# Two of the five wide combine passes of the sample stage on GpSimd instead of VectorE

## The reference

```python
def combine_patterns(outs, lses):
    w = jax.nn.softmax(jnp.stack(lses, axis=0), axis=0)
    return jnp.sum(w[..., None] * jnp.stack(outs, axis=0), axis=0)
```

## Time and profile before

| | |
|---|---|
| Runs | median 3155.96 us of 3 (3154.74 to 3160.87) |
| Profiled execution, its own time | 3153.91 us |
| Its span in the trace | 3152.2 us |
| Busy: PE, DVE, ACT, POOL | 91%, 39%, 28%, 6% of the span |

### The profile page before, as it was taken

One profiled execution on the slowest core, in us unless ns is written; L12 is line 12 of the kernel. 1 busy time (PEld: TensorE's weight loads), 2 busy tenths in 40 slices (PEclk: granted clock), 3 DMA queues, 4 the chain that ended last, 5 costly groups with the idle time before them and its releaser, 6 DMA issues. The chain is left out here.

```text
span 3152.2 us, 49398 instructions
## 1 busy us (share of the span) xinstructions
PE 2876.6 (91%) x17770; PEld 1632.3 (52%) x17770; DVE 1235.5 (39%) x2977; ACT 887.1 (28%) x2188; POOL 192.6 (6%) x476
## 2 busy tenths in 40 slices
PE   7998887673989898996997999999999999999998
PEld 6655665452657474765443444444444444444444
DVE  6326555564646465564443222222112221122134
ACT  6116666222434343443222110111001210011111
POOL 2000000100112020211110000000000000000000
PEclk9999889886989898997998999999999999999999
DMA  5121222752010201102322102111231112311035
GB/s 179 75 93 39 81 61 58 225 172 65 15 49 8 56 16 42 34 10 78 138 93 80 40 20 110 41 40 40 88 131 41 40 40 93 127 41 40 33 126 177
DMA packets 177965, 231.40 MB, mean 73 GB/s; under 512 B 12561, under 2 KB 141924, under 8 KB 177148
## 3 DMA queue, kind: packets, MB, share of 16 engines
q1 hardware_dynamic: 173142, 216.53, 21.4%
q0 software_dynamic: 4656, 12.65, 1.3%
HBM read 160.08 MB, written 69.07 MB: 73 GB/s over the span
## 5 line engine op out<-in xcount | busy, mean ns | idle before, releaser
L2312 DVE TENSOR_TENSOR f_hidden<-f_silu,f_ps_up 128x512 f32<-128x512 f32 (+1 forms) x110 | 65.2, 593 | 627.5 <-ACT f_silu L2253 627.5
L113 PE MATMUL f_ps_gate<-act_hi,f_w_hi 128*128 128x512 bf16 (+1 forms) x880 | 285.5, 343 | 11.1 <-DVE f_w_lo L2299 9.5
L113 PE MATMUL f_ps_y<-f_down_hi,f_h_hi 128*128 128x512 bf16 (+1 forms) x748 | 284.3, 380 | 8.5 <-issue 6.4
L114 PE MATMUL f_ps_gate<-act_lo,f_w_hi 128*128 128x512 bf16 (+1 forms) x880 | 285.4, 343 | 0.0
L115 PE MATMUL f_ps_gate<-act_hi,f_w_lo 128*128 128x512 bf16 (+1 forms) x880 | 285.2, 343 | 0.0
L114 PE MATMUL f_ps_up<-act_lo,f_w_hi 128*128 128x512 bf16 (+1 forms) x880 | 284.6, 342 | 0.0
L115 PE MATMUL f_ps_up<-act_hi,f_w_lo 128*128 128x512 bf16 (+1 forms) x880 | 284.6, 342 | 0.0
L113 PE MATMUL f_ps_up<-act_hi,f_w_hi 128*128 128x512 bf16 (+1 forms) x880 | 284.6, 342 | 0.0
L114 PE MATMUL f_ps_y<-f_down_lo,f_h_hi 128*128 128x512 bf16 (+1 forms) x748 | 284.3, 380 | 0.0
L115 PE MATMUL f_ps_y<-f_down_hi,f_h_lo 128*128 128x512 bf16 (+1 forms) x748 | 284.1, 380 | 0.0
L2253 ACT ACTIVATE f_silu<-f_ps_gate 128x512 f32<-128x512 f32 (+1 forms) x110 | 57.1, 519 | 656.6 <-PE f_ps_up L115 656.6
(11 more groups left out here) (360 smaller groups left out, 5483.0 us busy)
## 6 DMA issues: line engine op xcount, KB each, us to landing
y_part_rows<-f_total SPq DMA_DIRECT2D x48, 512.0 KB, 2.6
f_total<-y_part_rows SPq DMA_DIRECT2D x48, 512.0 KB, 3.5
f_raw_gate<-in_w_gate SPq DMA_DIRECT2D x22, 512.0 KB, 4.5
f_raw_up<-in_w_up SPq DMA_DIRECT2D x22, 512.0 KB, 5.9
f_raw_down<-in_w_down SPq DMA_DIRECT2D x22, 512.0 KB, 3.6
m_w_raw<-in_w_in SPq DMA_DIRECT2D x20, 512.0 KB, 5.1
s_comb<-pattern_rows SPq DMA_DIRECT2D x24, 396.0 KB, 4.4
nx<-in_x_prompt SPq DMA_DIRECT2D x16, 512.0 KB, 3.5
```

Of the source, the lines that this page charges most:

```text
L113: pe.matmul(out, w_hi, x_hi, start=first, stop=False)
L114: pe.matmul(out, w_hi, x_lo, start=False, stop=False)
L2312: nc.vector.tensor_tensor(hidden[u][:, 0:n], act_out[u][:, 0:n], ps_up[u][:, 0:n], ALU.mult).then_inc(hidden_done, 1)
```

## The change

Of the five wide passes of `combine(c)`, the two that multiply patterns 1 and 2 with their weights leave VectorE. GpSimd does them in place in `s_comb`, in a new function `scale(c)`, and raises a new semaphore `c_scaled` after each. VectorE still multiplies pattern 0, and its two adds wait for `c_scaled`. On GpSimd `scale(0)` and `scale(1)` stand behind the first two value loads, and each later `scale(b)` behind `values(b)`. The unchanged names of the semaphore list are cut here.

```diff
@@ -859,11 +859,21 @@
                     pool.dma_start(v[slot][0:DEC_SEQ, CACHE_TILES, :], g.kv_sample[ds(b * DEC_SEQ, DEC_SEQ), D_A:])\
                         .then_inc(v_in[slot], 16)
 
+                def scale(c):
+                    pool.wait_ge(c_weight_done, 4 * c + 2)
+                    for pat in (1, 2):
+                        num = comb[:, pat, :, 0:HD_A]
+                        nc.gpsimd.tensor_tensor(num, num, c_w[:, pat, :].unsqueeze(2).to_broadcast([P, BOTH, HD_A]),
+                                                ALU.mult).then_inc(c_scaled, 1)
+
                 values(0, 0)
                 values(1, 1)
+                scale(0)
+                scale(1)
                 for b in range(2, DEC_BATCH):
                     pool.wait_ge(o_ready, b - 1)
                     values(b, b % 2)
+                    scale(b)
 
             @block.tensor
             def _(pe):
@@ -1069,12 +1079,12 @@
                         dve.wait_ge(c_turned, 2 * c)
                     num = lambda pat: comb[:, pat, :, 0:HD_A]
                     wide = lambda pat: c_w[:, pat, :].unsqueeze(2).to_broadcast([P, BOTH, HD_A])
-                    nc.vector.tensor_tensor(c_out[:, :, :], num(0), wide(0), ALU.mult)
-                    nc.vector.tensor_tensor(num(1), num(1), wide(1), ALU.mult).then_inc(c_weight_done, 1)
-                    nc.vector.tensor_tensor(num(2), num(2), wide(2), ALU.mult)
+                    nc.vector.tensor_tensor(c_out[:, :, :], num(0), wide(0), ALU.mult).then_inc(c_weight_done, 1)
                     dve.wait_ge(c_weight_done, 4 * c + 3)
+                    dve.wait_ge(c_scaled, 2 * c + 1)
                     nc.vector.tensor_tensor(c_out[:, :, :], c_out[:, :, :], num(1), ALU.add).then_inc(c_weight_done, 1)
                     dve.wait_ge(c_weight_done, 4 * c + 4)
+                    dve.wait_ge(c_scaled, 2 * c + 2)
                     nc.vector.tensor_tensor(c_out[:, :, :], c_out[:, :, :], num(2), ALU.add).then_inc(c_done, 1)
```

More of the change, by code:

```diff
@@ L788, in stage_sample_attention @@
          s_ready, s_done, exp_done, rden_done, p_done, p_turned, p_kept, o_ready, o_kept, o_done, o_hi, o_lo,
-         mix_out, comb_in, c_min_done, c_diff_done, c_exp_done, c_part_done, c_weight_done, c_done, c_turned, c_high, c_low) = sems.new(
+         mix_out, comb_in, c_min_done, c_diff_done, c_exp_done, c_part_done, c_weight_done, c_done, c_turned, c_high, c_low, c_scaled) = sems.new(
             "s_k_in0", "s_k_in1", "s_v_in0", "s_v_in1", "s_bias_in", "s_k_turned", "s_big_hi", "s_small_hi",
@@ L793, in stage_sample_attention @@
             "s_mix_out", "s_comb_in", "s_c_min_done", "s_c_diff_done", "s_c_exp_done", "s_c_part_done", "s_c_weight_done",
-            "s_c_done", "s_c_turned", "s_c_high", "s_c_low")
+            "s_c_done", "s_c_turned", "s_c_high", "s_c_low", "s_c_scaled")
         k_in, v_in = [k_in0, k_in1], [v_in0, v_in1]
```

## The result

The change makes the kernel slower. Over eight runs of each, the median went from 3155.35 us to 3165.2 us; the ratio is 1.0029 with a 95% interval of 1.002 to 1.0038, that is 6 to 12 us. Timed again beside other kernels it was 1.0039 (1.0025 to 1.0052). The forecast was +16 us, 3171 us, in a range from 3158 to 3182.

A forecast was written before the change was run, and what follows sets the result against it. The prediction took the stage to be bound by TensorE waiting each turn for the end of `combine`. Eight combines, each +2.02 us with D = 1.8, gave +16.2 us: 3170.1 or 3172.2 us, given as 3171, range 3158 to 3182.

The forecast's parts named there:

- What bounds the stage: TensorE's `turn_out` waits for the end of `combine` in all 8 turns, 27.3 us; lengthening VectorE's wide passes costs in full.
- the tail: From the first wide pass of `combine` to `c_done`: 4.56 us before, 2.98 + 2D predicted after.
- the two engines don't work side by side: VectorE's instructions with two SBUF inputs shut out GpSimd's multiplies; chance 0.72, against 0.18 for running side by side.
- the add finds the second GpSimd pass running: In the tail, GpSimd's second pass follows its first without a wait, so VectorE's add meets it running.
- VectorE idles for about 2D: Sign in the profile after: VectorE idle between its multiply and its first add for two GpSimd passes.
- D: Length of one wide GpSimd multiply over 768 elements, taken as 1.8 us, between 1.46 and 2.10 with blocking.
- The length of a GpSimd pass: Bounded from memset rows: 0.83 us lowest, 1.46 for two reads in turn, 2.10 for three steps; 1.8 taken.
- The constant of the tail: The tail's part beside two GpSimd passes: 0.94 + 0.1 + 0.98 + 0.96 = 2.98 us.
- the forecast's own range: 3161 to 3180 us: 10.7 to 21.0 us for the tails, -5.8 to +3.1 us for TensorE's clock.
- The value loads: On GpSimd, moved behind `scale`: still in time for their matmuls, covered by 2.4 us and the shift; charged nothing.
- TensorE's clock: Lower clock level behind TensorE's wait: charged nothing, bounds -5.8 to +3.1 us over six turns.
- the first products: TensorE's first 14 matmuls of six turns, 16.6 us together; a changed length would mean the prediction is wrong.

The follow-up runs named there:

- one_pass: The change with only pattern 2 multiplied on GpSimd, VectorE keeping patterns 0 and 1; 1.0021 of the kernel before, +6.6 us.
- weight_psum: The change with pattern 0's weight first copied to PSUM, so VectorE's multiply has one SBUF input; 1.0018 of the kernel before.
- scalar_pass: The kernel before with pattern 2 multiplied on ScalarE in twelve instructions, one a head, none on GpSimd; 0.9989 of the kernel before, -3.5 us.
- loads_first: The change with the value loads of sample b + 1 issued ahead of GpSimd's passes of combine b; 1.0045 of the kernel before.
- early_gpsimd: The kernel before with combine's short operations and prepare's small casts moved earlier, and the change on top; 0.9977 of the kernel before.
- early_gpsimd_loads_late: early_gpsimd with value loads of samples 2 to 6 held until the next combine's pattern rows have landed; 0.9958 of the kernel before.

## Why the prediction was right

**What bounds the stage** held: TensorE waited for the end of `combine` in all eight turns, after as before, and with the weights where they were, each change of the tail came out in TensorE's wait in a turn: +0.96 us for a tail of +0.97 in the change, +0.52 for +0.52 in one_pass, +0.19 for +0.20 in weight_psum, -0.53 for -0.52 in scalar_pass.

**That the two engines don't work side by side** held, in both directions. VectorE first: 2.24 us for GpSimd's 1.46. GpSimd first, of which no row of before told: 2.15 us for VectorE's 0.95, and 2.23 in one_pass, where no semaphore stands between the two. The Trainium skill's rule in SBUF — State Buffer, "Who interferes with whom", says just this of a VectorE instruction with two SBUF inputs and a GpSimd instruction that reads SBUF; weight_psum shows the condition, since with one SBUF input fewer both kept their length. VectorE came first by 0.05 us only (614.10 against 614.15), since GpSimd started 0.08 us after the weights and not 0.16. In one point the prediction contradicts itself: it says that the add finds the second GpSimd pass running, and then that VectorE idles for about 2D. The trace has the first: VectorE idled 1.43 us, and the rest is inside the add's 2.15.

**The length of a GpSimd pass** was mis-sized: D = 1.46 us, not 1.8. It is the value that I had worked out for two reads one after the other with the write beside them; I took the middle between that and three steps. Over two passes and eight combines that is 5.4 us of the 16.2. The Trainium skill's figure for 2048 elements (GPSIMD Engine Reference, section 3.1), scaled to an estimate, gave 1.69, also too long; by it the sum was 14.4.

**The constant of the tail** was too large too: 2.98 us beside 2D, measured 5.53 - 2.92 = 2.61. If GpSimd's first pass worked for the last 1.46 us of its 2.24, it got going 0.83 us after VectorE's start (I had 0.94); the held add ended 0.82 us after GpSimd was through (I had 0.1 + 0.98); the last add took 0.99 (0.96); and the pair of passes 2.89 (2.92). So 0.26 of the 0.37 is the held add: with the semaphore already there, it needed less after its release than the 0.95 us of a free one. Why isn't shown. 8 x 0.37 = 3.0 us.

The two errors have one sign. With them the tails cost 7.8 us, which lies below the 10.7 to 21.0 that I gave for the tails: the mechanism was right and its price too high. Without the 5.8 us that the forecast's own range of 3161 to 3180 allows downward for the clock, its lower end would be 3166.7 and the measured 3165.2 below it. That the number lies inside is in part luck.

**The value loads** I charged at nothing, and asked only whether they themselves would be late. They were not: TensorE waits nowhere for `s_v` in the stage. But they now move at the same time as the pattern rows, and these land 2 us later (6.5 us for 4.4; 4.3 again in loads_first), which VectorE feels in the last combine, 1.5 us. The question that I left out was whom a moved transfer disturbs.

**TensorE's clock** I charged at nothing, with the sign that I would be wrong if the first products changed their length. They did, one by one: 2.25 us became 3.03, 3.08 became 2.28, 2.15 became 3.28, and all six together 17.4 us for 16.6, inside the bounds. But they don't hold all that moved. From the first to the seventh `turn_out` it was 696.22 - 580.62 = 115.6 us for 690.39 - 582.24 = 108.15, 1.6 us more than six tails; from the seventh to the eighth 15.47 for 12.46, 0.5 more than the tail and the rows; up to the first `turn_out` it was 22.2 for 21.9, 0.7 less than a tail adds, and from the eighth to the end of the stage 16.2 for 17.0, 0.8 less. The net is 0.7 us. That all of it is the clock isn't shown.

In sum: 16.2 - 5.4 - 3.0 + 1.5 + 0.7 = 10.0 us, for 9.9 in the stage. The 0.7 is what was left over, so the sum closes by construction; and that the medians of the runs also differ by 9.9 is close by chance, since the interval is 6 to 12.

## What to carry to other kernels

Before work is given to GpSimd beside VectorE, look at the inputs of what VectorE does in that time: beside instructions with two SBUF inputs the time of GpSimd's multiplies was added to VectorE's; beside those with one of the two inputs in PSUM it was free. An instruction that is recorded longer than its like may be held and not slow; its neighbour in time on the other engine tells. Here the gain lay in what stood ahead of the wide passes: eight short operations and the casts moved off the way to them gave 14 to 16 us where moving the wide passes cost about 10. And ask whom a moved transfer disturbs: the value loads weren't late, but the pattern rows were.

## What was not expected of the hardware

When VectorE comes upon two GpSimd passes that follow each other without a wait, it sometimes slips in between and sometimes not. In early_gpsimd it came 0.24 us before the end of the first and went next (1.05 us; GpSimd's second pass was then the one held). In early_gpsimd_loads_late it came 0.7 us after the first had begun (605.84 against 605.12) and waited for both, 3.02 us. The sum in the line is the same; what decides the turn is open.

ScalarE's twelve multiplies of 64 elements took 0.25 us each from start to start, 2.97 us for what VectorE does in 0.87 and GpSimd in 1.46.
